# Attention scores of a decoder layer: three terms over 64 rows in two row halves of the array

## The reference, cut to what matters

```
# 16 query heads, 4 key/value heads, head width 64, blocks of 128 tokens, window 128
scores = einsum('bnqkgd,bnskd->bnkgqs', qb, kw) * 64 ** -0.5   # kw: keys of this block and the one before
scores = where(allowed, scores, -inf)                          # 0 <= q_pos - k_pos < 128
probs  = softmax(concat([scores, sink]))[..., :-1]             # one learned sink logit per head
out    = einsum('bnkgqs,bnskd->bnqkgd', probs, vw)
```

## Time and profile before

| | us |
|---|---|
| runs, median (lowest to highest of 3) | 1271.7 (1267.66 to 1271.8) |
| span of the profiled execution | 1271.3 |
| PE busy | 1221.5 (96%) |
| DVE busy | 591.1 (46%) |
| ACT busy | 350.6 (28%) |
| POOL busy | 385.7 (30%) |
| mean granted TensorE clock | 0.987 of full speed |

### The profile page before, as it was taken

The page is one execution under the profiler, slowest core; times in us unless marked ns, Lnnn a source line. Parts: engine busy times, 40 slices in busy tenths (PEclk is TensorE's granted clock), DMA queues, the critical chain, the costliest instruction groups (busy, mean ns, idle before and its releaser), DMA issues.

```text
span 1271.3 us, 16160 instructions
## 1 busy us (share of the span) xinstructions
PE 1221.5 (96%) x5803; PEld 976.2 (77%) x5803; DVE 591.1 (46%) x1009; ACT 350.6 (28%) x857; POOL 385.7 (30%) x202
## 2 busy tenths in 40 slices
PE   5989999999999889999999999999999999899997
PEld 5777777777777668888778877887788778688886
DVE  4546745845835851034243523462256235744443
ACT  5622513413413430001232123312331134301221
POOL 4433133132222223344223422242233322332000
PEclk9999999999989989999999999999999999999999
DMA  5111121021021033521112111211111110554222
GB/s 186 51 34 37 30 67 50 18 66 49 16 67 48 20 105 123 165 83 50 34 35 67 50 34 34 82 39 43 33 58 57 49 33 33 198 185 146 100 82 82
DMA packets 101657, 87.19 MB, mean 69 GB/s; under 512 B 4980, under 2 KB 91120, under 8 KB 101616
## 3 DMA queue, kind: packets, MB, share of 16 engines
q1 hardware_dynamic: 97008, 69.88, 18.4%
q10 hardware_dynamic: 4608, 16.78, 3.6%
HBM read 69.87 MB, written 16.78 MB: 68 GB/s over the span
## 4 chain that ended last, share of the span: by engine, by line
PE 79%; DVE 9%; ACT 5%; DVEq 3%; issue 2%; DMA 0%; ACTq 0%; SPq 0%
PE ps L522 61%; PE ps L790 2%; PE ps L795 2%; PE ps L791 2%; ACT probs L932 2%; DVEq L1231 2%; DVE row_max L1232 1%; PE ps L740 1%; PE ps L730 1%; DVE u_lo L1297 1%; PE ps L615 1%; PE ps L734 1%; PE ps L744 1%; PE ps L727 1%; DVE probs L1226 1%
## 5 line engine op out<-in xcount | busy, mean ns | idle before, releaser
L522 PE MATMUL ps<-hT_hi,w_hi 128*128 128x512 f32 x1216 | 483.5, 398 | 5.7 <-DVE hT_lo L1423 3.7
L522 PE MATMUL ps<-hT_lo,w_hi 128*128 128x512 f32 x1216 | 480.4, 395 | 0.0
L522 PE MATMUL ps<-hT_hi,w_lo 128*128 128x512 f32 x1216 | 479.1, 394 | 0.0
L478 POOL TENSOR_TENSOR w_hi<-w_raw,zero_col 128x1024 fp32r<-128x1024 f32 x85 | 165.9, 1952 | 758.1 <-PE ps L522 732.4
L522 PEld LDWEIGHTS ps<-hT_hi,w_hi 128*128 128x128 f32 x1216 | 230.6, 190 | 56.2 <-issue 5.5
L522 PEld LDWEIGHTS ps<-hT_hi,w_lo 128*128 128x128 f32 x1216 | 230.3, 189 | 47.5 <-issue 1.4
L522 PEld LDWEIGHTS ps<-hT_lo,w_hi 128*128 128x128 f32 x1216 | 230.6, 190 | 46.7 <-issue 2.1
L480 POOL TENSOR_TENSOR w_lo<-w_raw,w_hi 128x1024 fp32r<-128x1024 f32 x84 | 212.4, 2529 | 11.9
L932 ACT ACTIVATE probs<-probs,neg_max 128x128 f32<-128x128 f32 x128 | 49.9, 391 | 115.9 <-DVE neg_max L1238 115.9
L1041 ACT ACTIVATE dmat<-ps,tok_gate 128x128 f32<-128x128 f32 x64 | 20.1, 364 | 191.8 <-PE ps L734 163.3
L1368 DVE SCALAR_TENSOR_TENSOR s_T<-ps,dmat 128x128 f32<-128x128 f32 x64 | 15.6, 285 | 100.6 <-ACT dmat L1041 100.6
(11 more groups left out here) (217 smaller groups left out, 1430.0 us busy)
## 6 DMA issues: line engine op xcount, KB each, us to landing
w_raw<-in_w_in SPq DMA_DIRECT2D x68, 512.0 KB, 3.8
branch_a_scratch<-ev ACTq DMA_DIRECT2D x16, 512.0 KB, 2.6
xs<-in_x SPq DMA_DIRECT2D x8, 512.0 KB, 5.1
w_raw<-in_w_branch_attn SPq DMA_DIRECT2D x8, 512.0 KB, 3.7
ev<-branch_a_scratch ACTq DMA_DIRECT2D x8, 512.0 KB, 3.8
tanh_gm_scratch<-ev ACTq DMA_DIRECT2D x8, 512.0 KB, 2.6
w_raw<-in_w_branch_mlstm SPq DMA_DIRECT2D x8, 512.0 KB, 7.8
th<-tanh_gm_scratch SPq DMA_DIRECT2D x8, 512.0 KB, 3.6
```

The source lines that it names most:

```text
L478: nc.gpsimd.tensor_tensor(hi, src, zero_col[:].to_broadcast(list(src.shape)), ALU.add)
L522: mm = nc.tensor.matmul(ps[:, 2 * s + b, :], w[:, k, :], r_[:, k, b * BANK:(b + 1) * BANK], start=(r == 0), stop=(r == KT * TERMS - 1))
```

## The change

The rounded and the rest part of q go into two tiles of 128 partitions, `q_hi` and `q_lo`, with both heads of a q tile in their own partition halves. ScalarE and VectorE then make each with one operation per q tile. The scores are three terms per head (q_hi·k_hi, q_hi·k_lo, q_lo·k_hi; the lo·lo term is left out), each over the 64 rows of the head's half. The two heads of a tile alternate between row halves and write to different banks. The heads in PSUM and in the probabilities now stand in the order 0, 2, 1, 3, so the sinks are permuted once by VectorE, and P·V takes two neighbouring heads instead of every second one.

```
-        act: for r in range(2):
-                 A(q_split[0:64, 2*j+r, :], dense_ps(S2+j)[rows, :], Identity, bias=...).then_inc(q_hi_ready, 1)
+        act: A(q_hi[:, j, :], dense_ps(S2+j), Identity, bias=...).then_inc(q_hi_ready, 1)

-        dve: for h in range(GR):
-                 V.scalar_tensor_tensor(q_split[64:128, h, :], dense_ps(S2+j)[rows, :], bias,
-                                        q_split[0:64, h, :], ALU.add, ALU.subtract)
+        dve: for j in range(2):
+                 V.scalar_tensor_tensor(q_lo[:, j, :], dense_ps(S2+j), bias, q_hi[:, j, :], ALU.add, ALU.subtract)

     def scores(n):
         first = max(n - 1, 0)
-        for h in range(GR):
-            o = ps[:, X[h // 2], (h % 2) * 2 * P + (P if n == 0 else 0):(h % 2 + 1) * 2 * P]
-            for part in (k_hi, k_lo):
-                mm = nc.tensor.matmul(o, q_split[:, h, n * P:(n + 1) * P], part[:, first * P:(n + 1) * P],
-                                      start=(part is k_hi), stop=(part is k_lo))
+        for j in range(2):
+            terms = ((q_hi, k_hi), (q_hi, k_lo), (q_lo, k_hi))
+            for term, (q, k) in enumerate(terms):
+                for r in range(2):
+                    rows = slice(64 * r, 64 * r + 64)
+                    o = ps[:, X[r], j * 2 * P + (P if n == 0 else 0):(j + 1) * 2 * P]
+                    mm = nc.tensor.matmul(o, q[rows, j, n * P:(n + 1) * P], k[rows, first * P:(n + 1) * P],
+                                          start=(term == 0), stop=(term == 2))

-        P·V: pT_cur[:, r:GR:2, :], pT_prev[:, r:GR:2, :]
+        P·V: pT_cur[:, 2*r:2*r+2, :], pT_prev[:, 2*r:2*r+2, :]

+        dve, once, between the gate sums and the wait for ScalarE's logarithm:
+            dve.wait_ge(bias_in, 16 * 3)
+            V.tensor_copy(sink_tab[:].rearrange("p (g r j) -> p g j r", r=2, j=2),
+                          sink_raw[:].rearrange("p (g j r) -> p g j r", r=2, j=2))
```

More of the change, by code:

```diff
@@ L126, in build @@
         sink_tab = sb("sink_tab", [P, HEADS])
+        sink_raw = sb("sink_raw", [P, HEADS])
         zero_col = sb("zero_col", [P, 1])
@@ L168, in build @@
             [("k_dup", [P, KV, T]), ("v_tok", [P, NB, KV * HD]), ("k_hi", [P, T], F32R), ("k_lo", [P, T], F32R), ("v_head", [P, NB, HD]),
-             ("q_split", [P, GR, T], F32R), ("silu_z", [P, 2, T]),
+             ("q_hi", [P, 2, T], F32R), ("q_lo", [P, 2, T], F32R), ("silu_z", [P, 2, T]),
              ("probs0", [P, GR, P]), ("probs1", [P, GR, P]), ("pT_cur", [P, GR, P]), ("pT_prev", [P, GR, P])],
@@ L177, in build @@
             [("under_merged", [P, KT, T]), ("wo_raw", [P, KT, T])]])
-        k_dup, v_tok, k_hi, k_lo, v_head, q_split, silu_z, probs0, probs1, pT_cur, pT_prev = att
+        k_dup, v_tok, k_hi, k_lo, v_head, q_hi, q_lo, silu_z, probs0, probs1, pT_cur, pT_prev = att
         probs = [probs0, probs1]
@@ L231, in build @@
         q_hi_ready = sem("q_hi_ready")
-        q_split_ready = sem("q_split_ready")
+        q_lo_ready = sem("q_lo_ready")
         kv_head_ready = sem("kv_head_ready")
@@ L339, in _ @@
             sp.dma_start(gate_bias[32:40, :], b_in[MF0:MO0].rearrange("(h a) -> h a", a=1)).then_inc(bias_in, 16)
-            sp.dma_start(sink_tab[:, :], sinks.partition_broadcast(P)).then_inc(bias_in, 16)
+            sp.dma_start(sink_raw[:, :], sinks.partition_broadcast(P)).then_inc(bias_in, 16)
             def weights(t0, tiles):
@@ L661, in attention_step @@
                             o = ps[64 * r:64 * r + 64, X[3], 0:2 * P]
-                            mm = nc.tensor.matmul(o, v_head[:, m, :], pT_cur[:, r:GR:2, :], start=True, stop=(m == 0))
+                            heads = slice(2 * r, 2 * r + 2)
+                            mm = nc.tensor.matmul(o, v_head[:, m, :], pT_cur[:, heads, :], start=True, stop=(m == 0))
                             if m:
-                                mm = nc.tensor.matmul(o, v_head[:, m - 1, :], pT_prev[:, r:GR:2, :], start=False, stop=True)
+                                mm = nc.tensor.matmul(o, v_head[:, m - 1, :], pT_prev[:, heads, :], start=False, stop=True)
                         mm.then_inc(pv_done, 1)
@@ L900, in attention_step @@
                     act.wait_ge(tile_done, t0 + 1 + j)
[L901 to L905, removed]
+                    A(q_hi[:, j, :], dense_ps(S2 + j), ACT.Identity, bias=par[:, ds(R_Q + j + 2 * g, 1)])\
+                        .then_inc(q_hi_ready, 1)
+                    act.wait_ge(q_lo_ready, 2 * g + j + 1)
                     act.sem_inc(tile_out, 1)
@@ L1209, in attention_step @@
                 V.tensor_copy(v_head[:], v_tok[:, :, ds(HD * g, HD)]).then_inc(kv_head_ready, 1)
[L1211 to L1216, removed]
+                for j in range(2):
+                    dve.wait_ge(q_hi_ready, 2 * g + j + 1)
+                    V.scalar_tensor_tensor(q_lo[:, j, :], dense_ps(S2 + j), par[:, ds(R_Q + j + 2 * g, 1)],
+                                           q_hi[:, j, :].bitcast(F32), ALU.add, ALU.subtract).then_inc(q_lo_ready, 1)
                 def combine(n):
```

## The result

The changed kernel takes 1273.1 us, the kernel before 1270.49 us (medians of 18 runs each): ratio 1.0017, 95% interval 1.0009 to 1.0024, or about +2.2 us (the two medians lie 2.6 us apart). The forecast was +2.6 us, 1274 us on the base of the first three runs. The measured difference is inside the 0.5% that counts as no change, and clear of zero.

The account below looks back on a forecast made before the run. TensorE was taken as the bound (79% of the chain of waits). Six blocks at +0.15 us less 0.26 for q give +0.65 us a group, +2.6 in four: 1271.7 + 2.6, say 1274 us; range 1263 to 1284.

Parts of the forecast that it names:

- The periods: Score blocks: twelve 64-row matmuls run side by side in pairs, six periods of 0.12 us, 0.72 us a block.
- The price of the shape: Around each score block: changing array shape in and out, with loads in the open, costs 0.39 us a block.
- Rival A: Score blocks: row halves don't overlap, +0.8 us a block, 1278 to 1297 us; chance 0.15.
- Rival B: Score blocks: the change of shape is hidden, only the shorter periods count, -6.8 us, 1265 us; chance 0.10.
- Rival D: Score blocks: array not cut, 12 full-shape matmuls, +0.48 us a block, -4 to +14 us; chance 0.08.
- The q split: Ahead of block 0's scores: one operation per q tile on ScalarE and VectorE removes a stall, -0.26 us a group.
- What is hidden: Blocks 2 and 5 pay inside stalls; the other six add 0.15 us each, 0.9 us a group.
- the time around the span: Outside the profiled span: 0.4 us, kept unchanged in the forecast time.
- Rival C: Group end: slower scores delay GpSimd's split past VectorE's operation, shrinking the stall; -1 to -9 us, about 1266; chance 0.15.

Follow-up runs that it names:

- e1: The changed kernel without the score matmuls of the odd heads, 6 of 12 a block left out; ratio 1.0011 to the kernel before.
- e4: The changed kernel with q_hi and q_lo made head by head again, in operations of 64 partitions; ratio 1.0009 to the kernel before.
- e2: The changed kernel with two score terms instead of three (q_lo times k_hi left out); ratio 0.9979 to the kernel before.
- e3: The changed kernel with one dense matmul moved between the two head pairs of each score block; ratio 0.9983 to the kernel before.
- e5: The kernel before, with GpSimd's first weight split behind a group waiting until VectorE has scaled the last probabilities; 1253.38 us, ratio 0.9862.
- e6: The changed kernel with the same GpSimd wait as e5; 1256.71 us, ratio 0.9891 to the kernel before.
- e7: e5 plus waits on the low halves of the two GpSimd splits inside a group, for probabilities of blocks 1 and 4; 1245.73 us, ratio 0.9797.
- e8: The changed kernel with the three GpSimd waits of e7; 1249.87 us, ratio 0.9829 to the kernel before.
- e11: The changed kernel with score matmuls issued head by head, three terms of one head then three of the other; ratio 1.0021 to the kernel before.

## Why the prediction was right

**The periods** (six of 0.12 us for twelve matmuls): right, shown by the starts and by e1. **The price of the shape** (0.09 + 0.10 + 0.09 + 0.11 us): right to 0.01 in each of the four terms, though read from a 40-row and a 64-column matmul of the mLSTM. **Rival A** is out: the third pair of a block has the row halves of the second and starts 0.12 us after it, not 0.23. The Trainium skill (TensorE: Matmul & The Clock Gate, The mechanism) says that a load overlaps matmuls in flight only in another row group; the measurement decides against this for this shape. **Rival B** is out: the change of shape is paid in full. The halves double the rate of the matmuls alone, 12 in the time of 6, and not of the block: 1.11 us of 12 half matmuls against 0.96 us of 8 whole ones. The Trainium skill (TensorEngine Tiling (Array Packing), Theoretical Speedup) gives up to twofold, and the trace agrees for the matmuls alone. **Rival D** is out by the pairs.

**The q split**: the gap went in groups 1 to 3, as predicted. I booked it as 0.26 us and block 0 as 0.15 us; e4 shows 0.17 and the starts show that block 0 pays less, so that the two together come out as booked, at about -0.11 us.

**What is hidden**: blocks 2 and 5 are, as predicted (e2 and e3 show it from block to block), but the sum over the rest was mis-sized. I took six blocks of 0.15 a group on the path, +0.65 us with q. The period went from 88.22 us (e5) to 88.62 us (e6), +0.40, with the end-of-group stall out of the way, where I had said it doesn't hide anything. The starts of the score blocks tell why. From block 0 to block 1 the changed kernel takes only 0.05 us more (4.67 against 4.62), and from 6 to 7 0.09 more (6.40 against 6.31). Blocks 0 and 6 came after a wait in the kernel before, and so probably had part of the first load in the open already. For block 6 the pair e7 and e8, without that wait, bears this out: there it pays 0.16 us. From 5 to 6 it is 0.08 less. Blocks 1, 3 and 4 paid 0.15 to 0.16, block 2 nothing. That is 0.53 us up to block 7 and 0.15 in it, less 0.26: +0.42. Four groups: 1.7 us, and 0.26 more in group 0, which had no q gap: 1.9 us. Measured: 2.2 us (1.1 to 3.0). So the forecast of 2.6 us held although a term of it was half as large again as what was measured (0.65 against 0.42).

**Luck** has a part in how well it held. The forecast has no term for the clock, and the clock was not equal: at one clock the difference would be about 3.6 us by the estimate above, of which the starts explain 1.9. The remaining 1.7 us are traced to nothing, and may be the estimate's own error: in group 1 the low stretch behind the stall cost only about 0.7 us (48.92 us from block 7 to the next block 0, against 48.09 us in the changed kernel, where 0.11 of the difference is the change's own, by e5 and e6). A small reading was wrong as well: the time around the span is 1.7 us (1270.7 and 1269.0 for the changed kernel's profiled run) and not 0.4 us, which compared the span of one run with the median of others. It cancels in the difference.

**Rival C** was a true mechanism, and the changed kernel stopped short of it. I had the split 0.30 us later and 0.20 short; it came 0.18 us later and stopped 0.32 short. Taken in proportion, its decisive point lies nearer +0.4 us a block (an estimate) than the +0.25 that I gave; at e3's +0.54 both 128x4 operations were free. I had counted 1.8 us a group for the stall and up to 1.4 for the clock; the stall alone is worth 3.4 us a group (e6). What e3 got back from it was less, since the scaling of probs then met the split (2.46 us instead of 0.69).

**Left open**: why a stall is followed by 1.2 GHz in one execution and not in another, and the 1.7 us above. No experiment held the clock fixed.

## What to carry to other kernels

Cutting the array in row halves doubles the rate of 64-row matmuls, but entering and leaving that shape costs 0.39 us; a block needs to save at least four periods of 256 columns (0.12 us each, an estimate from the 0.39) to pay for it, or neighbours of a cut shape to share the change with. When two engines meet by phase (here VectorE and GpSimd), a small slowdown elsewhere can take a stall away (e3), so look for the meeting and pin it with a wait: one wait on GpSimd brought 1.4% and three 2.0%, about ten times what the change moved. Test a change of this size on the kernel with the stalls removed, where its own cost (here 4.1 us between e7 and e8) isn't hidden, and compare periods at equal clock beside the times.

## What the hardware showed unexpectedly

- A VectorE operation of 128x4 elements, 0.16 us when free (e3), took 2.36 us when GpSimd's split was running (the changed kernel, at 254.13). Others inside a split kept their time: in e7 the merge into probs, which reads PSUM (0.73 us at 228.42, in the split from 227.45 to 230.76), and the maximum over probs (0.69 us at 209.84, in the split begun at 209.19). The split begun at 227.45 took 3.31 us itself, where the one at 209.19 took 2.40; a 1.22 us operation of VectorE had started at 227.29.
- Matmuls for the two row halves ran in pairs, starts 0.01 us apart, although three for one half were issued ahead of the other's (e11).
- A stall of 2.7 us was followed by 1.2 GHz in all four groups of one execution of the kernel before and in one of four of the changed kernel's, with the stalls of equal length. Between executions of the changed kernel the span moved by 5.5 us with the mean clock (1268.3 us at 0.994, 1273.8 us at 0.986).
- The best version, e7, is 2.0% faster than the kernel before, at 1245.7 us, without the change that this study is about.
